# An output projection in two halves, an up projection with one token group first, and GpSimd passes cut in two

## The reference, cut to what matters

```python
yl = concat([hgrn2(al), chunk_mlp(pl[u], pl[v])], -1) @ w_out    # even_mixer; yc the same for the context
xl = xl + g1 * yl
h  = rms_norm(xl, norm_ffn_w) * (1 + sc2) + sh2
up = h @ w_up                      # gate and value, 2816 each
xl = xl + g2 * ((silu(conv3(gate)) * value) @ w_down)
# chunk_mlp: u * (ws @ rms_norm(gelu(v)) + bs)
```

## Time and profile before

| | |
|---|---|
| time, median of 3 runs | 2578.45 us (2570.19 to 2580.16) |
| the profiled execution: time, span | 2579.7 us, 2577.9 us |
| mean granted TensorE clock | 0.956 |
| TensorE matmuls busy | 2451.1 us (95%) |
| DVE, ScalarE, GpSimd busy | 1023.3, 894.9, 864.7 us (40%, 35%, 34%) |
| GpSimd's weight passes (L460) | 267, 625.5 us |

### The profile page before, as it was taken

One profiled execution on the slowest core, in us unless ns is written; L12 is line 12 of the kernel. 1 busy time (PEld: TensorE's weight loads), 2 busy tenths in 40 slices (PEclk: granted clock), 3 DMA queues, 4 the chain that ended last, 5 costly groups with the idle time before them and its releaser, 6 DMA issues.

```text
span 2577.9 us, 36722 instructions
## 1 busy us (share of the span) xinstructions
PE 2451.1 (95%) x14405; PEld 2035.1 (79%) x14405; DVE 1023.3 (40%) x1669; ACT 894.9 (35%) x1387; POOL 864.7 (34%) x527
## 2 busy tenths in 40 slices
PE   6999999987999999999999999999999999999997
PEld 3876976976888888888887778888887886688766
DVE  4762673144233223334223236322345004752173
ACT  5433343233222222324411344222344225633462
POOL 2453364223222222323231214444444441134302
PEclk9999999998999999999877899999999999999999
DMA  7177168111212211212210002233332321122211
GB/s 279 59 267 271 50 245 327 62 49 41 61 61 65 65 58 64 65 58 70 75 34 1 1 17 82 90 98 94 94 98 74 127 97 62 51 66 82 72 49 66
DMA packets 56952, 234.92 MB, mean 91 GB/s; under 512 B 6336, under 2 KB 7616, under 8 KB 56064
## 3 DMA queue, kind: packets, MB, share of 16 engines
q1 hardware_dynamic: 56592, 232.44, 26.7%
q0 software_dynamic: 240, 0.79, 0.1%
HBM read 231.11 MB, written 2.10 MB: 90 GB/s over the span
## 4 chain that ended last, share of the span: by engine, by line
PE 85%; DVE 6%; ACT 3%; DMA 2%; POOL 2%; issue 2%; SPq 0%; DVEq 0%; ACTq 0%; POOLq 0%
PE ps L849 16%; PE ps L850 15%; PE ps L851 15%; PE ps L1477 4%; PE ps L1479 4%; PE ps L1480 4%; PE ps L1298 2%; PE ps L602 2%; PE ps L1371 2%; DMA XB<-ada_dram 2%; PE ps L1673 1%; PE ps L1660 1%; PE ps L1597 1%; PE ps L886 1%; PE ps L887 1%
## 5 line engine op out<-in xcount | busy, mean ns | idle before, releaser
L460 POOL TENSOR_TENSOR w_low<-ring,w_high 128x1024 fp32r<-128x1024 f32 (+2 forms) x267 | 625.5, 2344 | 1308.9 <-ACT w_high L453 1308.9
L453 ACT ACTIVATE w_high<-ring 128x1024 fp32r<-128x1024 f32 (+2 forms) x267 | 274.6, 1032 | 987.7 <-PE ps L851 653.0
L849 PE MATMUL ps<-h_high,w_high 128*128 128x512 f32 x1040 | 411.5, 396 | 12.7 <-DVE h_low L705 9.0
L850 PE MATMUL ps<-h_low,w_high 128*128 128x512 f32 x1040 | 408.6, 393 | 0.0
L851 PE MATMUL ps<-h_high,w_low 128*128 128x512 f32 x1040 | 407.7, 392 | 0.0
L849 PEld LDWEIGHTS ps<-h_high,w_high 128*128 128x128 f32 x1040 | 197.4, 190 | 60.1 <-DVE h_low L705 9.9
L851 PEld LDWEIGHTS ps<-h_high,w_low 128*128 128x128 f32 x1040 | 197.3, 190 | 42.0
L850 PEld LDWEIGHTS ps<-h_low,w_high 128*128 128x128 f32 x1040 | 197.6, 190 | 38.4
L1477 PE MATMUL ps<-hidden,w_high 128*128 128x512 f32 (+1 forms) x504 | 178.6, 354 | 0.0
L1479 PE MATMUL ps<-hidden,w_high 128*128 128x512 f32 (+1 forms) x504 | 178.5, 354 | 0.0
L1480 PE MATMUL ps<-hidden,w_low 128*128 128x512 f32 (+1 forms) x504 | 178.3, 354 | 0.0
(11 more groups left out here) (443 smaller groups left out, 5144.6 us busy)
## 6 DMA issues: line engine op xcount, KB each, us to landing
XB<-ada_dram SPq DMA_DIRECT2D x84, 768.0 KB, 6.0
ring<-up_dram SPq DMA_DIRECT2D x88, 512.0 KB, 3.6
ring<-down_dram SPq DMA_DIRECT2D x44, 512.0 KB, 3.6
ring<-winE_dram SPq DMA_DIRECT2D x32, 512.0 KB, 3.3
ring<-win_dram SPq DMA_DIRECT2D x20, 512.0 KB, 3.6
ring<-winC_dram SPq DMA_DIRECT2D x20, 512.0 KB, 3.3
arena<-ada_dram SPq DMA_DIRECT2D x12, 768.0 KB, 21.1
XB<-xl_dram SPq DMA_DIRECT2D x2, 2048.0 KB, 9.5
```

Of the source, the lines that this page charges most:

```text
L453: nc.scalar.activation(WH[p][:, 0:L], RAW[p][:, 0:L], ACT.Copy).then_inc(w_hi, 1)
L460: nc.gpsimd.tensor_tensor(WL[p][:, 0:L], RAW[p][:, 0:L], WH[p][:, 0:L].bitcast(F32), ALU.subtract)\
L849: nc.tensor.matmul(bank[:, 0:n], wh[:, cols], hi, start=(k == 0), stop=False)
L850: nc.tensor.matmul(bank[:, 0:n], wh[:, cols], lo, start=False, stop=False)
```

## The change

- The parts of Y get places of their own (`y_part`): tiles 0 to 3 in the buffer of the layer's inputs, 4 to 7 behind the gating stage's work. ScalarE rounds tiles 0 to 3 between `mlp_values(0)` and the copy of wmlp's chunk 6, DVE takes their low parts before its own waits for the values. Tiles 4 to 7 are parted one by one as each is finished.
- `project_both`: chunks 0 and 1 are gone through twice, first with tiles 0 to 3 for both segments, then with tiles 4 to 7; chunks 2 to 7 as before.
- In the norms n1, n3, n5, n6 the last tile's squares are not added on DVE; TensorE sums SA (seven tiles) and the last squares apart. In `out_squares` the copy of the next stage's chunk 1 goes behind the last squares.
- n1: both inversions ahead of the scaling. The first up round is taken out of TensorE's loop: chunks 0 and 1 for the latent tokens, chunks 0 and 1 for the context, then chunks 2 and 3 as before.
- Each `split_lo` is two instructions over half the columns; the semaphore comes with the second.

```diff
@@ split_lo
-            nc.gpsimd.tensor_tensor(WL[p][:, 0:L], RAW[p][:, 0:L], WH[p][:, 0:L].bitcast(F32), ALU.subtract)\
-                .then_inc(raw_spent[p], 1)
+            for at in range(0, L, L // 2):
+                to = slice(at, at + L // 2)
+                ins = nc.gpsimd.tensor_tensor(WL[p][:, to], RAW[p][:, to], WH[p][:, to].bitcast(F32), ALU.subtract)
+            ins.then_inc(raw_spent[p], 1)
@@ mean
-            tiles_ = [KT - 1] if stage in ADDED else range(1, KT, 2) if (stage, k) in PAIRED else range(len(srcs))
+            tiles_ = [KT - 2, KT - 1] if stage in LAST_APART else [KT - 1] if stage in ADDED else range(1, KT, 2) if (stage, k) in PAIRED else range(len(srcs))
...
-                if stage in ADDED:
+                if stage in ADDED and not (stage in LAST_APART and j == KT - 1):
@@ scale_parted
-            if stage != "n0":
+            if stage not in ("n0", "n1"):
                 invert(stage, k)
@@ TensorE, ffn
                 if norm in DEFERRED:
                     unscaled_two(pe, norm)
...
+                else:
+                    for s in segs:
+                        for c in range(2):
+                            split_features(pe, up, c, up, ns * c + s, KT, P, h_parts(norm), (s,),
+                                           ready=h_there(pe, norm) if c == 0 else None)
+                for c in range(2, 4):
+                    split_features(pe, up, c, up, ns * c, KT, P, h_parts(norm), segs,
+                                   ready=h_there(pe, norm) if c == 2 and norm in DEFERRED else None)
+                with pe.Fori(1, FT // 2) as i:
@@ TensorE, in place of project_out("wout0", ...)
+                for half in range(2):
+                    for c in range(2):
+                        wh, wl = await_parts(pe, "wout0", c)
+                        for s, (a, n) in enumerate(SEGS):
+                            bank = bank_ap("wout0", 2 * c + s) if half else open_bank(pe, "wout0", 2 * c + s)
+                            for k in range(KT // 2 * half, KT // 2 * (half + 1)):
+                                if c == 0 and s == 0:
+                                    pe.wait_ge(y_lo, k + 1)
...
+                            if half:
+                                sums_done(ins, "wout0", 2 * c + s)
+                for c in range(2, KT):
+                    split_features(pe, "wout0", c, "wout0", 2 * c, KT, P, parted_, (0, 1))
@@ ScalarE
             mlp_values(0)
+            act.wait_ge(part_lo, 4 * KT)
+            for k in range(KT // 2):
+                A(y_part(k, 0), Y[:, k, :], ACT.Copy).then_inc(y_hi, 1)
             split_hi("wmlp", 6)
...
-            act.wait_ge(y_ready, 1)
-            y_high(Y, YH0, T)
+            for k in range(KT // 2, KT):
+                act.wait_ge(y_ready, k - KT // 2 + 1)
+                A(y_part(k, 0), Y[:, k, :], ACT.Copy).then_inc(y_hi, 1)
@@ ScalarE, out_squares
-                    split_hi(stage, k + 2) if k + 2 < KT else after and split_hi(after, k + 2 - KT)
+                    if k < KT - 1:
+                        split_hi(stage, k + 2) if k + 2 < KT else after and split_hi(after, k + 2 - KT)
...
+                if after:
+                    split_hi(after, 1)
@@ DVE
+            for k in range(KT // 2):
+                both_low(k)
             for g in range(5, 10):
                 await_taken(dve, "wmlp", g)
...
-            ins.then_inc(y_ready, 1)
+                ins.then_inc(y_ready, 1)
+                if q:
+                    both_low(KT // 2 + q - 1)
+            both_low(KT - 1)
...
-                        if k >= 2:
+                        if 2 <= k < KT:
                             add_square(norm, s, k - 1)
...
-            y_low(Y, YH0, YL0, T, 0)
             dve.wait_ge(x_in, 64)
             add_out("wout0", (0, 1), lambda k, s: mod[:, 0, 16 + k, s:s + 1], "n1")
+            for s in range(2):
+                invert("n1", s)
```

More of the change, by code:

```diff
@@ L148 @@
 ADDED = ("n0", "n1", "n3", "n5", "n6")
+LAST_APART = ADDED[1:]
 PAIRED = (("n2", 0), ("n4", 0))
@@ L255, in two_blocks @@
         UNS = {x: [parts(f"unscaled{x}{j}", ARENA_AT + at, KT, 2, U_HALF) for j, at in enumerate(ats)] for x, ats in U_AT.items()}
-        YH0, YL0 = (parts(f"y{x}_both", ARENA_AT + x * KT * T, KT, T) for x in (1, 2))
+        WK_AT = 18 * T
+        YP = parts("y_first", H_AT, 2, KT // 2, T)
+        YQ = parts("y_last", ARENA_AT + WK_AT + 7 * S, 2, KT // 2, T)
         YH, YLo = (parts(f"y{x}", ARENA_AT + x * KT * S, KT, S) for x in (0, 1))
-        WK_AT = 18 * T
         IN_W0 = parts("in_parts_w0", ARENA_AT + WK_AT, 7, S)
@@ L530, in last_square @@
         def last_square(stage, k, j):
-            return stage not in ADDED and k == batches(stage)[batch_of(stage, k)][-1] and j == len(ITEMS[stage][k][0]) - 1
+            last = k == batches(stage)[batch_of(stage, k)][-1] and j == len(ITEMS[stage][k][0]) - 1
+            return last and (stage not in ADDED or stage in LAST_APART)
         def item_width(stage, k):
@@ L924, in in_part, with y_part @@
             return place[:, a:a + CTX]
+        def y_part(k, low_):
+            return (YQ if k >= KT // 2 else YP)[:, low_, k % (KT // 2), :]
         def in_parts(x):
@@ L1448, in ffn @@
                     unscaled_two(pe, norm)
-                    for c in range(2, 4):
-                        split_features(pe, up, c, up, ns * c, KT, P, h_parts(norm), segs,
-                                       ready=h_there(pe, norm) if c == 2 else None)
-                with pe.Fori(norm in DEFERRED, FT // 2) as i:
+                else:
[7 more added lines that the diff above has]
+                with pe.Fori(1, FT // 2) as i:
                     for c in range(4):
-                        split_features(pe, up, c, up, ns * c, KT, P, h_parts(norm), segs, loops=i, pairs=2 * i,
-                                       ready=h_there(pe, norm) if c == 0 and norm not in DEFERRED else None)
+                        split_features(pe, up, c, up, ns * c, KT, P, h_parts(norm), segs, loops=i, pairs=2 * i)
                 for x in range(2):
@@ L1493, in ffn, with project_both @@
                     hidden(RUN - 1, 0, False, True)
-            project_out("wout0", YH0, YL0, (0, 1), 0)
+            def project_both():
+                parted_ = lambda s, k: tuple(y_part(k, x)[:, SEGS[s][0]:sum(SEGS[s])] for x in range(2))
+                for half in range(2):
[6 more added lines that the diff above has]
+                                    pe.wait_ge(y_lo, k + 1)
+                                hi, lo = parted_(s, k)
+                                cols = slice(k * P, (k + 1) * P)
+                                MM, to = nc.tensor.matmul, bank[:, 0:n]
+                                MM(to, wh[:, cols], hi, start=(k == 0), stop=False, skip_group_check=True)
+                                MM(to, wh[:, cols], lo, start=False, stop=False, skip_group_check=True)
+                                ins = MM(to, wl[:, cols], hi, start=False, stop=(k == KT - 1), skip_group_check=True)
+                            if half:
+                                sums_done(ins, "wout0", 2 * c + s)
+                for c in range(2, KT):
+                    split_features(pe, "wout0", c, "wout0", 2 * c, KT, P, parted_, (0, 1))
+            project_both()
             means(pe, "n1")
@@ L2175, in _ @@
             for k in range(KT // 2, KT):
-                act.wait_ge(y_ready, k - 2)
+                act.wait_ge(y_ready, k + 1)
                 A(YH[:, k, :], HL[:, k, :], ACT.Copy).then_inc(y_hi, 1)
@@ L2524, in _, with both_low @@
             step.settle()
+            def both_low(k):
+                dve.wait_ge(y_hi, k + 1)
+                TT(y_part(k, 1), Y[:, k, :], y_part(k, 0).bitcast(F32), ALU.subtract).then_inc(y_lo, 1)
+            for k in range(KT // 2):
+                both_low(k)
             for g in range(5, 10):
```

## The result

| | before | changed |
|---|---|---|
| time, median | 2574.32 us | 2541.81 us |
| its runs | 2567.89 to 2580.16 (4) | 2536.35 to 2551.59 (4) |
| profiled execution: time, span | 2579.7, 2577.9 us | 2551.59, 2549.8 us |
| mean granted clock there | 0.956 | 0.966 |

The ratio is 0.9877 with a 95% interval of 0.9846 to 0.9909: 31.7 us faster (23.4 to 39.6). The forecast was 22.0 us and 2556.5, its range 2548 to 2567. One execution of a later kernel (the one with the gap doubled) took 4301.45 us at a mean clock of 0.75 and is left out of its median.

A forecast was written before the change was run, and what follows sets the result against it. TensorE, busy in 95% of the span, was taken as the bound, so only its waits and half-clock stretches count. Terms summed to -22.0: profiled 2579.7 to 2557.7, median 2556.5 us; 8-in-10 range 2548 to 2567.

The forecast's parts named there:

- The projection, -10.5: First output projection: its first half starts right behind the gating matmuls, ending at 594.9 instead of 605.44; 10.5 us gained.
- Rival (c): Projection's second half waits because collisions with passes of wout0 push low parts back: 6.9 gained, 2560 us; chance 0.08.
- (d): Projection's early start is given back, by copies delaying chunk 6 of wmlp or by held weights: 2570 us; chance 0.05.
- Norm 1's end, -3.3: After the projection: means and spread sooner, first scaled tile at 611.35 instead of 614.66; 3.3 us gained.
- Rival (a): The lower clock stays through norm 1 and first up, which keep 3 instead of 10 us: 2563 us; chance 0.17.
- First up, -6.7: First up projection: first scaled tile to third chunk in 23.1 instead of 29.8 us, with a 1.15 us stall; 6.7 gained.
- z: Start of norm 1's first scaled tile, from which the forecast counts the first up projection's times.
- Halves at the norms, -2.8: Norms n2 to n5: halved GpSimd passes free the shared port 1.2 us sooner for low parts; 2.8 us gained.
- at 1963.90 and 2273.97, -2.0: Two places on TensorE's path where halved passes free the port sooner: 1.0 us each, 2.0 gained.
- rival (b): Port not handed over at the half, the second half being already queued: 4.8 gone, 0.8 paid, 2562 us; chance 0.10.
- Losses of the halves, +2.1 and +0.6: Longer halved passes: 2.1 us lost in the recurrent rounds and three other waits, 0.6 at the short chunks.
- Rival (e): Slower: GpSimd's halved pass sets TensorE's pace everywhere, 2594 to 2604 us; chance 0.03.

The follow-up runs named there:

- gap doubled: Changed kernel with two more vector copies ahead of the one TensorE's first attention sum waits for (idle 1.40 to about 2.9 us): 2553.73 us, ratio 0.9933.
- Before without the gap: Kernel before, with only the second attention sum waiting for the vector copies out of the Fourier sums, removing 1.40 us of TensorE idle: 2566.66 us, 0.9964.
- quarters: Changed kernel with short passes whole, the Fourier-copy wait moved to the second attention sum, and long passes in quarters of 256 columns: 2555.16 us, 0.9941.

## Why the prediction was right and wrong

- **The projection, -10.5**: measured -10.4 or -10.5 in all eight kernels with it. First matmul without a wait, second half without a wait, full clock. Rival (c) is out, and (d) too: of ScalarE's 6.12 us of idle time ahead of the copy for wmlp's chunk 6 the four roundings take 3.05 and leave 3.19, and that copy stands at the same distance ahead of the gating matmuls in all sixteen profiles, within 0.1 us.
- **Norm 1's end, -3.3**: measured -2.4 (7.06 for 9.50). The means ran at full clock as assumed, the spread did not: a matmul each 0.21 us instead of 0.12. Rival (a) is half true: 10 of the 20 us at the lower clock remain, but norm 1 and up gained 8.9, not the 3 that it left them.
- **First up, -6.7**: measured -6.6, the third chunk at z + 23.2 for z + 23.1, its new stall 0.88 for 1.15.
- **Halves at the norms, -2.8, and at 1963.90 and 2273.97, -2.0**: the port is handed over at the half, rival (b) is out. The low part took 1.58 for 1.5, a pass of 512 columns 1.36 in the mean for 1.26. At n4 the gain was 2.8 for 1.7. 1.9 of it stand at the two chunks on unscaled inputs: the wait there fell from 1.86 to 0.57 us, and the half-clock stretch behind it from 7 us to 3. Another 1.1 come with the low parts. (Before without the gap, with no halves, gained 1.1 there by the shorter stretch alone, so this part can come without the change.) The wait and the clock behind it in before (timeline, window):

```profile
1965.79 0.38 PE L777 MATMUL ps<-unscaledn,w_high 128*128 128x256 f32 x1 [1.86 <-DVE unscaledn L759]
...
1966.00:1976.00 10.00, 10.00 (x61) 10.00 (x61) 0.51 (x3) 1.21 (x2) 3.23 (x2) 0.66 0.31 107
```

And in the changed kernel:

```profile
1942.36 1.05 PE L607 MATMUL ps<-const,SQ 128*128 128x1 f32 x8 [0.57 <-POOL SQ L517]
...
1943.00:1953.00 10.00, 9.29 (x63) 8.95 (x62) 4.01 (x9) 3.90 (x7) 3.15 (x3) 0.83 0.25 88
```

- **Losses of the halves, +2.1 and +0.6**: the recurrent pass lost 0.57 where I had 0.83; TensorE's two waits for such passes grew by 0.8 together, for the 2.1 of the forecast, while the effect on the time is not resolved, as the part ahead of the gating matmuls varies by 12 us between profiles (+7.3 in the changed kernel's first, -5.0 in before's second). The short chunks cost 1.0 to 1.5 for 0.6, and the second block's attention 1.2 for 0. Rival (e) is out: passes of 2.72, even of quarters, never set the pace of the feed-forward.
- **The step that failed** is the sum's frame. I priced the clock in the two places that the change touches, and took every other stage as it stood in the one profiled execution. So the sum has 0 for all stages that the edit does not reach. In that execution 20 us at the lower level stood at the start of the attention sums, and 3 us more at woutM; the changed kernel has neither, and by stages that is worth 8.0 us and 1.8, as much as the 9.7 between forecast and result. The errors of the other stages are smaller and nearly cancel: 1.4 to 2.1 more than forecast at n2, 1.1 at n4, 1.2 at the head norms, 0.3 to 1.5 in the last layer, against 1.6 to 3.2 less at nB, 1.1 to 1.3 less at norm 1 and up and 1.2 less in the attention ahead of nB. The page's row of granted clock does not show the stretch: its low digits (8, 7, 7) are in the main the stages ahead of it, and stand in the changed kernel's page as well. A window of 20 us shows it, and the 1.40 us wait ahead of it was among TensorE's waits; I read neither, since the change does not come near them.

Against before's executions of high mean clock the changed kernel is 21.8 us faster, and its stages sum to -24.0 and -22.2 against before's second profile, where the forecast has -24.1: that agreement is of sums, not of each stage, and in part luck. What is shown is that the stretch at the attention hangs on this gap: without it there is none, with twice the gap it stands in a kernel that had none. What stays open is why the same 1.40 to 1.44 us is followed by it in four of eleven profiles and not in the others, and whether the change itself keeps the changed kernel clear of it (nine of ten executions have the high mean clock) or only a shift of time that it brings along; which shift was not found.

## What to carry to other kernels

Read TensorE's granted clock along the whole span, not only at the edit, and list each wait that stands just ahead of a stretch at the lower level: such a wait can cost six times its length, and any edit upstream can switch it on or off. Where a stretch comes and goes between executions of the same kernel, make the sum against both courses. Move a semaphore wait behind the first work that does not need it. Whether two short waits are better than one of their length is only hinted at here, by the one profile with quarters; look at the clock behind a wait before you merge it with another. And take more than one profile of a kernel before you put a difference in clock down to an edit.

## What was not expected of the hardware

- 1.46 us more of idle TensorE cost 11 us in one kernel, and 1.40 less gave 9.3 in another: after the gap the granted clock was 0.50 to 0.54 for 17 to 20 us in which the engine was busy without pause. Yet in seven of eleven profiles a gap of 1.40 to 1.44 us at the same place had no such stretch behind it.
- At n2, two waits of 0.83 and 1.41 us were followed by at most 3 us at the lower clock in seven profiles (in one by none), a single one of 2.76, in one profile, by 13 us, with nearly the same work around them.
- The Trainium skill ("SBUF — State Buffer", Who interferes with whom) has a vector instruction with two SBUF inputs and a GpSimd instruction exclude each other for the whole instruction. The trace agrees: before, the vector engine's low part at n3 took 2.66 us beside a whole pass, and ended 0.55 us behind it. It also shows the exchange: 65.7 us more of GpSimd's busy time (608.5 to 674.2 for the long passes) for 36.5 less of the vector engine's (changed kernel with whole passes against halves).
